# Reordering the weight units of three FFN output products: two-tile unit first in each half

## The reference, cut to what matters

```
h = (silu(gate) * value)            # 256 tokens x 2816 features
f = h @ w_down                      # 2816 x 1024: the FFN output product
x = x + gate_f * f                  # first block ("down")
x = x + rms_norm(f, gain)           # second block, twice ("g0" and "g1")
```

## Time and profile before

| what | value |
|---|---|
| median of 3 runs | 1211.2 us (1208.37 to 1214.16) |
| profiled execution, its own time | 1211.38 us |
| its span, first to last instruction | 1210.1 us |
| mean granted TensorE clock | 0.974 of full speed |
| PE busy | 1151.7 us, 95% |
| DVE busy | 749.3 us, 62% |
| ACT busy | 600.7 us, 50% |
| HBM read | 205.52 MB |

### The profile page before, as it was taken

How to read it: one execution, slowest core, us unless ns; L and a number is a source line. 1 busy time by engine, 2 the same in 40 slices (tenths; PEclk the granted TensorE clock), 3 DMA queues, 4 the chain that set the end, 5 groups by cost and what they waited for, 6 DMA issues and landing times.

```text
span 1210.1 us, 19204 instructions
## 1 busy us (share of the span) xinstructions
PE 1151.7 (95%) x7762; PEld 1036.4 (86%) x7762; DVE 749.3 (62%) x1408; ACT 600.7 (50%) x1060; POOL 31.0 (3%) x32
## 2 busy tenths in 40 slices
PE   6899999899899999999998999999999999999998
PEld 3777989788779999888987799998878878999976
DVE  4655477788658788765466656665454446666644
ACT  2344466445456666445444564444464346544532
POOL 0411000000000000001000000000000000000000
PEclk9898999899899999999999999999999989999999
DMA  8757173245134555564542275554534304655450
GB/s 356 306 212 314 53 270 140 95 186 218 60 139 158 179 190 189 191 248 154 186 149 102 87 270 186 175 180 175 183 130 150 105 32 145 224 174 183 149 191 35
DMA packets 30508, 207.81 MB, mean 172 GB/s; under 512 B 3507, under 2 KB 4019, under 8 KB 6612
## 3 DMA queue, kind: packets, MB, share of 16 engines
q1 hardware_dynamic: 30420, 206.58, 47.1%
HBM read 205.52 MB, written 1.05 MB: 171 GB/s over the span
## 4 chain that ended last, share of the span: by engine, by line
PE 82%; DVE 9%; ACT 5%; issue 3%; DMA 1%; SPq 0%; ACTq 0%; DVEq 0%
PE ps L391 49%; PE ps L1527 18%; PE ps L409 2%; DVE wlo L350 2%; ACT whi L343 1%; PE ps L2144 1%; PE ps L2112 1%; DVE tm L558 1%; PE ps L1226 1%; ACT sq L1542 1%; PE ps L519 1%; PE ps L1304 1%; PE ps L755 1%; PE ps L1009 1%; DMA raw<-ada 1%
## 5 line engine op out<-in xcount | busy, mean ns | idle before, releaser
L350 DVE TENSOR_TENSOR wlo<-raw,whi 128x1024 fp32r<-128x1024 f32 x324 | 371.3, 1189 | 245.1 <-ACT whi L343 245.1
L391 PE MATMUL ps<-H_h,whi 128*128 128x256 f32 x1648 | 475.4, 288 | 4.1 <-DVE H_l L503 3.1
L391 PE MATMUL ps<-H_h,wlo 128*128 128x256 f32 x1648 | 469.3, 285 | 0.0
L391 PE MATMUL ps<-H_l,whi 128*128 128x256 f32 x1648 | 469.2, 285 | 0.0
L343 ACT ACTIVATE whi<-raw 128x1024 fp32r<-128x1024 f32 x324 | 315.0, 1022 | 154.9 <-PE ps L1527 111.8
L391 PEld LDWEIGHTS ps<-H_h,whi 128*128 128x128 f32 x1648 | 319.5, 194 | 9.2 <-issue 7.2
L391 PEld LDWEIGHTS ps<-H_l,whi 128*128 128x128 f32 x1648 | 319.6, 194 | 0.5 <-issue 0.2
L391 PEld LDWEIGHTS ps<-H_h,wlo 128*128 128x128 f32 x1648 | 319.2, 194 | 0.0
L1527 PE MATMUL ps<-whi,gl_h 128*128 128x512 f32 x264 | 105.3, 399 | 0.5 <-DVE wlo L350 0.5
L1527 PE MATMUL ps<-wlo,gl_h 128*128 128x512 f32 x264 | 104.3, 395 | 0.0
L1527 PE MATMUL ps<-whi,gl_l 128*128 128x512 f32 x264 | 104.3, 395 | 0.0
(11 more groups left out here) (416 smaller groups left out, 1421.7 us busy)
## 6 DMA issues: line engine op xcount, KB each, us to landing
raw<-f SPq DMA_DIRECT2D x44, 1024.0 KB, 4.9
raw<-win SPq DMA_DIRECT2D x33, 1024.0 KB, 6.3
raw<-ada SPq DMA_DIRECT2D x24, 1024.0 KB, 5.5
raw<-up SPq DMA_DIRECT2D x22, 1024.0 KB, 4.9
raw<-g SPq DMA_DIRECT2D x20, 1024.0 KB, 4.9
raw<-pw SPq DMA_DIRECT2D x12, 1024.0 KB, 4.9
raw<-down SPq DMA_DIRECT2D x10, 1024.0 KB, 5.7
raw<-ck SPq DMA_DIRECT2D x4, 1024.0 KB, 7.1
```

The source lines that it names most:

```text
L350: dve.tensor_tensor(wlo[j % NS][:, a:b], raw_of(key)[:, a:b], whi[j % NS][:, a:b].bitcast(F32), ALU.subtract).then_inc(w_lo.hit(key, half), 1)
L391: ins_ = pe.matmul(bank[:, m * 256:(m + 1) * 256], wt[a][:, kt * w + col + m * 128:kt * w + col + m * 128 + 128], act[b][:, k0 + kt, :], s ...
```

## The change

The unit of two tiles comes first in each half of "down", "g0" and "g1" in place of last. The tile ranges become 0-1, 2-5, 6-9, 10-13, 14-17, 18-21, where they were 0-3, ..., 16-19, 20-21. The number of units, tiles, matmuls and bytes is the same, and so is every other line. The last unit, in which t = 0 runs ahead of t = 1, has four tiles in place of two.

```diff
-WIDE, WIDER = [(4, 512)] * 4, ([(4, 512)] * 5 + [(2, 512)]) * 2
+WIDE, WIDER = [(4, 512)] * 4, ([(2, 512)] + [(4, 512)] * 5) * 2
...
-    k22 = [(4 * j, min(4 * j + 4, 22)) for j in r(6)]
+    k22 = [(max(4 * j - 2, 0), 4 * j + 2) for j in r(6)]
```

## The result

| | before | after |
|---|---|---|
| median | 1210.84 us (1208.37 to 1214.16, 6 runs) | 1223.61 us (1222.43 to 1225.16, 6 runs) |
| ratio | | 1.0103, 95% interval 1.0084 to 1.0121 |
| profiled execution, span | 1210.1 us | 1222.2 us |
| mean granted clock | 0.974 | 0.970 |
| PE busy | 1151.7 us | 1157.4 us |

The changed kernel is 12.8 us slower by the medians. The forecast was slower by 8.4 us with a range up to 1222.6 us, so direction and main mechanism were right, and the size was outside the range.

The account below looks back on a forecast made before the run. PE, busy 95% of the span, was taken as the bound, so order matters only where it stands still. Waits less ends, +4.65 us, and the clock, +3.8 us, gave +8.4 us: 1219.6 us, range 1214.8 to 1222.6.

Parts of the forecast that it names:

- The way to unit 1 of g0 and g1: Starts of g0 and g1: unit 1 gets ready no earlier while unit 0 is shorter, +2.8 us in each.
- The two longer waits of down: In down, PE waits 1.05 us for unit 1 at the start and 1.2 us for unit 8 after the change of halves.
- the change of halves: Middle of each stage: 0.4 us of cover left for unit 7, nothing lost; if that failed, some 0.1 us a stage.
- the ends: Stage tails start earlier against PE's last matmul: -1.6 us in g0, -1.25 in down, -0.6 in g1.
- Rival B: Starts of g0 and g1: same waits, clock holds in one stage (1217.7 us) or both (1215.8 us); chance 0.30.
- rival C: Starts of g0 and g1: unit 1 is not late, only the ends count, -3.45 us, 1207.8 us; chance 0.08.
- rival D: Short waits of down lower the clock too, 1.55 us for each of the two longer ones, 1222.7 us; chance 0.06.
- The clock: Behind the long waits of g0 and g1 the clock falls to 0.50: 1.9 us each, +3.8 us, between 0 and 5.4.
- the dense row's 1.55: Profile row at 963.8, dense matmuls following a 2.2 us wait: 3.4 us at clock 0.50 cost 1.55 us.
- Waits less ends: Sum without the clock over down, g0 and g1: 2.8 + 2.8 + 1.3 + 1.2 - 1.6 - 1.25 - 0.6 = +4.65 us.

Follow-up runs that it names:

- down_only: The kernel before with the two-tile unit first in down alone, g0 and g1 as before: 1219.54 us, ratio 1.0042.
- before_delay5: The kernel before with five more idle matmuls between the transposes of t = 0 and t = 1 ahead of mix0: 1216.84 us, ratio 1.0027.
- after_hold: The changed kernel with six idle matmuls in PE's wait between unit 0 and unit 1 of g0 and of g1: 1219.29 us.
- after_delay4: The changed kernel with four more idle matmuls ahead of the second transposes before mix0: 1223.99 us.
- g_only: The kernel before with the two-tile unit first in g0 and g1 alone, down as before: 1217.32 us, ratio 1.0037.

## Why the prediction was wrong in size

**Right.** The order only matters where PE stands still. The way to unit 1 of g0 and g1 didn't move, and 12 matmuls moved behind it: 2.79 us measured with the clock held, 2.8 forecast. The two longer waits of down came where they were put, 1.13 at the start and 1.30 us at unit 8, behind the finished columns. No wait came at the change of halves in g0 or g1. At the ends PE's own idle matmuls became the bound. The clock fell behind both long waits in both traces of the changed kernel and held when they were filled: shown. Rival B (the clock holds) and rival C (unit 1 comes earlier) are out; so is rival D, as the short waits of down left the clock at 1.00. For these two waits the trace does not bear out what the Trainium skill ("TensorE: Matmul & The Clock Gate", "A second HAM failure mode: psum-queue depth-cycling") says of small idle gaps; the falls in mix0, behind gaps of 0.36 and 0.62 us, look more like it, though no run shows that they are the same thing.

**The step that failed** is the one named "The clock". It priced falls only directly behind the two new waits ("+3.8 us for the two stages") and took the stages that the change doesn't touch to be the same. down ends 1.5 us later, and mix0 then had the 0.50 stretch with 4.6 us in all five traces in which mix0 began 1.3 to 1.5 us later than by the old order and had no idle matmuls (the changed kernel twice, down_only, before_delay5, after_hold); at 3.2 us later (after_delay4) it cost 3.0 us. The kernel before had it in one of three, at 3.0 us, and g_only once, at 3.1 us. The profiled execution of the kernel before happened to be without it, and it was the only one read; that its three executions lay 5.8 us apart was left unexplained. Had mix0's little matmul work been noted as thin, a rival with 3 to 5 us for it would have held the result in its range.

**Terms mis-sized.** The clock behind the waits cost 1.4 and 1.5 us, not 1.9: the dense row's 1.55 was the right one. down's PE part took 3.25 us in place of 2.5. Counted from the start of one matmul to the start of the next, PE lost 1.39 us at unit 1, 0.29 at unit 2 and 1.57 at unit 8, where 1.05, 0.25 and 1.2 were forecast. The idle in brackets is only 1.13, 0.03 and 1.30 us: a wait costs some 0.27 us more than it shows. The trace counts idle from the end of the matmul before, but without a wait the next one starts 0.17 us ahead of that end; and the second matmul behind a wait starts 0.33 us after the first in place of 0.23. The forecast had the same 0.17 us in its starting point, since it took down's start from the chain (491.44, the end of the matmul before) and not from the timeline (first matmul at 491.28). The ends gave 4.5 us in place of 3.45 for the same reason, the other way round: without a wait the transposes of g0 start 0.17 us ahead of the end of the idle matmuls (896.13 + 6.21 = 902.34, transposes from 902.17), and the two waits taken away showed 1.64 us and gave 2.17 in g0, 1.25 and 1.78 us in down.

**Luck.** Waits less ends came to 4.4 us, near the forecast's 4.65, because two errors offset each other: the waits cost 0.7 us more and the ends gave 1.0 us more than forecast.

**Sum.** By the stages of the traces, of 12.8 us 4.4 are waits less ends, 4.6 come with mix0 against an execution without the fall there, and 2.9 with the clock in g0 and g1; the rest, about 1 us, is within the spread of the medians. Against the average of the kernel before, which has a shorter fall in mix0 in some executions, mix0's share is less than 4.6; how much less the traces are too few to say.

**Open.** Why the fall in mix0 comes so surely at +1.3 to +1.5 us, also once at -1.8 us, and in a part of the executions at 0 was not settled. That the thin stretch brings it is shown by the idle matmuls in it: none of six traces with them has the fall, nine of eleven without them have. They also move the work behind them by 0.4 us; that this shift does it was not tested by itself, but shifts of -1.8, +1.3, +1.5 and +3.2 us all had the fall in their traces. The spread of the head and of mix1 was not studied.

## What to carry to other kernels

A short work unit is placed by what has to be ready behind it. At the start of a stage it uncovers the preparation of the next unit, which hangs on the stage ahead; last, it leaves the tail no time; in the next-to-last place it costs nothing and the tail gets its long unit. And where a wait of some 3 us or a thin stretch of small matmuls stands between dense ones, look at the granted clock over several executions, also in stages the change doesn't touch: a shift of 1.5 us cost more there than any wait it came from.

## What the runs showed of the hardware

The clock fell without any long wait: in mix0 PE stood for no more than 0.62 us at a time (0.36 and 0.62 us, the first among matmuls of 8 columns), and in nine of eleven traces 6.7 to 10.2 us at 0.50 followed; three more matmuls of 256 columns in those gaps held it at 1.00 in six traces. Behind the same 3.06 us wait the low stretch was 3.4 us in both traces of the changed kernel and 6.7 us in g0 of g_only (2.8 us of cost in place of 1.4). And filling a wait changes nothing of the wait, but won 2.9 us.
